# Two layers of a diffusion trunk on one Trainium2 core: where experts stand in the passes, how tokens are gathered, and which ScalarE tables are loaded

## What is computed

```python
def hier_moe(h, w_rg, b_rg, w_re, b_re, w_g, w_u, w_d):      # x: 256 tokens x 1024
    g_prob = softmax(x @ w_rg + b_rg); p_group, g_idx = top_k(g_prob, 1)          # 4 groups
    e_in = the 8 logits of (x @ w_re + b_re) in that group
    top_p, top_i = top_k(softmax(e_in), 2)                                        # 2 experts of 8
    gates = one_hot(ids) * (top_p / sum(top_p) * p_group)                         # 256 x 32
    hid = silu(einsum("nd,edf->nef", x, w_g)) * einsum("nd,edf->nef", x, w_u)     # f = 256
    y = einsum("nef,efd->nd", hid * gates[:, :, None], w_d)
```

## Time and profile before

| | us |
|---|---|
| median of 3 runs | 956.28 (954.70 to 958.65) |
| the profiled execution | 955.08 |
| its span, first to last instruction | 953.3 |
| PE busy | 824.9 (87%) |
| DVE busy | 350.6 (37%) |
| ACT busy | 203.9 (21%) |
| POOL busy | 37.5 (4%) |
| moved by DMA | 291.60 MB, mean 306 GB/s |

### The profile page before, as it was taken

The page is one execution under the profiler, slowest core; times in us unless marked ns, Lnnn a source line. Parts: engine busy times, 40 slices in busy tenths (PEclk is TensorE's granted clock), DMA queues, the critical chain, the costliest instruction groups (busy, mean ns, idle before and its releaser), DMA issues.

```text
span 953.3 us, 17639 instructions
## 1 busy us (share of the span) xinstructions
PE 824.9 (87%) x7754; PEld 550.4 (58%) x7754; DVE 350.6 (37%) x682; ACT 203.9 (21%) x360; POOL 37.5 (4%) x33
## 2 busy tenths in 40 slices
PE   4799999889996999898786789999599988978665
PEld 3687676778896464363343264898546444533324
DVE  0255567224236434232423231233543432341323
ACT  2215222233351111111111040304121111111103
POOL 0000010101004000000000000000400000000000
PEclk9999999999997999899988889999599998998886
DMA  9973345849994998999999999820089799999931
GB/s 341 378 262 108 111 139 206 299 179 282 398 402 192 371 379 323 414 417 414 419 413 419 393 386 395 353 89 1 0 350 388 314 415 418 414 420 413 418 159 45
DMA packets 88591, 291.60 MB, mean 306 GB/s; under 512 B 10857, under 2 KB 13887, under 8 KB 72127
## 3 DMA queue, kind: packets, MB, share of 16 engines
q1 hardware_dynamic: 77984, 284.70, 76.2%
q10 hardware_dynamic: 10527, 5.73, 2.1%
HBM read 288.31 MB, written 2.10 MB: 305 GB/s over the span
## 4 chain that ended last, share of the span: by engine, by line
PE 65%; DMA 21%; SPq 5%; DVE 4%; ACT 2%; issue 2%; ACTq 1%; DVEq 0%
DMA ring<-in_w_exp_up 14%; PE psum L1197 13%; PE psum L1121 6%; PE psum L798 6%; DMA scratch<-in_w_exp_up 5%; PE psum L1215 5%; PE psum L830 4%; PE psum L1187 4%; PE psum L1226 4%; PE psum L888 3%; PE psum L744 3%; PE psum L1323 3%; PE psum L1336 3%; SPq L606 2%; DMA ring<-in_w_in_even 2%
## 5 line engine op out<-in xcount | busy, mean ns | idle before, releaser
L1197 PE MATMUL psum<-scratch 128*32 128x512 f32 (+2 forms) x528 | 151.9, 665 | 32.6 <-DMA ring<-in_w_exp_up 26.4
L1197 PE MATMUL psum<-ring,scratch 128*32 128x512 f32 (+2 forms) x528 | 134.8, 656 | 23.1 <-DMA scratch<-in_w_exp_up 19.3
L1197 PEld LDWEIGHTS psum<-scratch 128*32 128x32 f32 (+2 forms) x528 | 43.9, 136 | 111.8 <-issue 111.7
L1226 PE MATMUL psum<-scratch 128*128 128x256 bf16 x576 | 70.4, 281 | 9.8 <-DVE scratch L2195 9.8
L1197 PEld LDWEIGHTS psum<-ring,scratch 128*32 128x32 f32 (+2 forms) x528 | 38.2, 129 | 69.2 <-issue 69.2
L1226 PEld LDWEIGHTS psum<-scratch 128*128 128x128 bf16 x576 | 56.3, 101 | 36.1 <-issue 16.9
L1187 PE MATMUL psum<-scratch 128*128 128x128 bf16 x1152 | 73.0, 227 | 2.7 <-DVE scratch L2179 2.7
L1187 PEld LDWEIGHTS psum<-scratch 128*128 128x128 bf16 x1152 | 70.8, 102 | 3.0 <-issue 2.8
L1652 ACT ACTIVATE scratch<-psum 128x256 f32<-128x256 f32 x24 | 9.2, 384 | 261.0 <-PE psum L1197 261.0
L798 PE MATMUL psum<-hT,ring 128*128 128x256 f32 x256 | 57.4, 387 | 2.4 <-DMA ring<-in_w_in_even 2.4
L2199 DVE TENSOR_TENSOR scratch<-psum,scratch 128x256 f32<-128x256 f32 x24 | 10.2, 424 | 125.1 <-ACT scratch L1652 125.0
(11 more groups left out here) (313 smaller groups left out, 1039.9 us busy)
## 6 DMA issues: line engine op xcount, KB each, us to landing
ring<-in_w_mod SPq DMA_DIRECT2D x42, 1024.0 KB, 8.8
scratch<-in_w_exp_gate SPq DMA_DIRECT2D x32, 1024.0 KB, 15.9
scratch<-in_w_exp_up SPq DMA_DIRECT2D x32, 1024.0 KB, 18.1
scratch<-in_w_exp_down SPq DMA_DIRECT2D x32, 1024.0 KB, 21.1
ring<-in_w_exp_gate SPq DMA_DIRECT2D x32, 1024.0 KB, 17.4
ring<-in_w_exp_up SPq DMA_DIRECT2D x32, 1024.0 KB, 18.9
ring<-in_w_exp_down SPq DMA_DIRECT2D x28, 1024.0 KB, 20.4
ring<-in_w_in_even SPq DMA_DIRECT2D x14, 1024.0 KB, 15.0
```

The lines of the kernel that those rows point to most:

```text
L1197: last = mm(bank[0][i * m:(i + 1) * m, :], xg[:, k, i * m:(i + 1) * m], w[e][:, k, :, :], start=(k == 0), stop=(k == KT - 1))
L1226: last = mm(bank[4 + k // 2][:, (k % 2) * T:(k % 2 + 1) * T], y3[:, j, k, :], ohT, start=False, stop=True, skip_group_check=True)
```

## The change

- NFIX goes from 4 to 6: experts 0 to 5 have fixed places in the first three pairs. The order of the passes changes from pair, pair, mono, quad, pair, quad, pair, three, pair, quad, pair, quad to pair, pair, pair, quad, pair, pair, quad, mono, quad, pair, three, quad. All 32 experts are still loaded, in 49 chunks; SP waits for the router ahead of q == 3.
- The gather multiplies float32 rows (hrow) by a float32 one-hot matrix: 8 matmuls for each half. The second copy on ACT and all of POOL's splitting are gone.
- ACT loads one common table for Ln and Exp (roots), and Silu's or Gelu's ahead of their use (gates, preload_act_table). Line numbers shift by a few; those of the profile before are used here.

```diff
-NFIX = 4
+NFIX = 6
-RANK2 = 10
+RANK2 = 8
-PASSES = [("pair", [("e", 0), ("e", 1)], 0), ("pair", [("e", 2), ("e", 3)], 4), ("mono", [("r", 0)], 8),
-          ("quad", [("r", 12 + i) for i in range(4)], 32), ("pair", [("r", 1), ("r", 2)], 12),
-          ("quad", [("r", 16 + i) for i in range(4)], 36), ("pair", [("r", 3), ("r", 4)], 16),
-          ("three", [("r", 9), ("r", 10), ("r", 11)], 28), ("pair", [("r", 5), ("r", 6)], 20),
-          ("quad", [("r", 20 + i) for i in range(4)], 40), ("pair", [("r", 7), ("r", 8)], 24),
-          ("quad", [("r", 24 + i) for i in range(4)], 44)]
+PASSES = [("pair", [("e", 0), ("e", 1)], 0), ("pair", [("e", 2), ("e", 3)], 4), ("pair", [("e", 4), ("e", 5)], 8),
+          ("quad", [("r", 10 + i) for i in range(4)], 32), ("pair", [("r", 1), ("r", 2)], 16),
+          ("pair", [("r", 3), ("r", 4)], 20), ("quad", [("r", 14 + i) for i in range(4)], 36), ("mono", [("r", 0)], 12),
+          ("quad", [("r", 18 + i) for i in range(4)], 40), ("pair", [("r", 5), ("r", 6)], 24),
+          ("three", [("r", 7), ("r", 8), ("r", 9)], 28), ("quad", [("r", 22 + i) for i in range(4)], 44)]
...
-                    if q == 2:
+                    if q == NFIX // 2:
                         sp.wait_ge(S.v_pos, 3 * l + 3)
...
-                        for j in range(3):
-                            last = mm(bank[b][:, k * P:(k + 1) * P], h3[j][:, t, half * 4 + k, :], Pm[:, t, :],
-                                      start=(t == 0 and j == 0), stop=(t == 1 and j == 2))
+                        last = mm(bank[b][:, k * P:(k + 1) * P], hrow[:, t, half * 4 + k, :], Pm[:, t, :],
+                                  start=(t == 0), stop=(t == 1))
...
-                pe.wait_ge(S.g_h, 6 * l + 6)
...
+            def roots():
+                nc.scalar.preload_act_table_set("natural_log_exp_and_others")
+            def gates():
+                nc.scalar.preload_act_table(ACT.Silu)
...
+            gates()
             gate_silu(6)
             columns_copy(0, 5)
             columns_copy(1, 4)
             gate_silu(7)
+            roots()
             columns_copy(2, 5)
...
-                    A(hrow[:, t, :, at], src, ACT.Copy)
-                    A(h3[0][:, t, :, at], src, ACT.Copy).then_inc(S.a_hr, 1)
+                    A(hrow[:, t, :, at], src, ACT.Copy).then_inc(S.a_hr, 1)
...
+            roots()
             act.wait_ge(S.t_ws, 1)
             A(wsT[:, :, :].rearrange("p g n -> p (g n)"), bank[4], ACT.Copy).then_inc(S.a_ws, 1)
...
-            for l in range(DEPTH):
-                for t in range(NB):
-                    n = 6 * l + 3 * t
-                    pool.wait_ge(S.a_hr, 4 * l + 2 * t + 2)
-                    nc.gpsimd.tensor_tensor(hrow[:, t], hrow[:, t], h3[0][:, t], ALU.subtract).then_inc(S.g_h, 1)
-                    pool.wait_ge(S.g_h, n + 1)
-                    pool.tensor_copy(h3[1][:, t], hrow[:, t]).then_inc(S.g_h, 1)
-                    pool.wait_ge(S.g_h, n + 2)
-                    nc.gpsimd.tensor_tensor(h3[2][:, t], hrow[:, t], h3[1][:, t], ALU.subtract).then_inc(S.g_h, 1)
```

More of the change, by code:

```diff
@@ L195, in __init__ @@
         self.g_bm = sem("g_bm")
-        self.g_h = sem("g_h")
         self.g_v1 = sem("g_v1")
@@ L433, in build @@
         bsp = part(10240, (4, P))
-        hrow = part(0, (NB, KT, P))
         xg = part(0, (KT, 2 * CAP))
@@ L441, in build @@
         pgT = part(2816, (T,))
-        Pm = scratch[:, 3072:3200].bitcast(BF16).rearrange("p (t s) -> p t s", t=NB)
-        ohT = scratch[:, 3200:3200 + T // 2].bitcast(BF16)
+        Pm = part(3072, (NB, 2 * CAP))
+        ohT = scratch[:, 10144:10144 + T // 2].bitcast(BF16)
         PG = part(3328, (NB, 2 * CAP))
@@ L448, in build @@
         R0 = 6688
-        h3 = [scratch[:, at:at + NB * D // 2].bitcast(BF16).rearrange("p (t k n) -> p t k n", t=NB, k=KT)
-              for at in (8096, 9120, 10144)]
+        hrow = part(8096, (NB, KT, P))
         more = [scratch[:, 11360 + i * SLOT:11360 + (i + 1) * SLOT] for i in range(MORE)]
@@ L1696, in layer_norm_scale @@
                     A(vsq, vtk[:, t, :], ACT.Square, accum_out=lns[:, t:t + 1]).then_inc(S.a_sqv, 1)
+                roots()
                 act.wait_ge(S.a_sqv, 2)
                 inv_root(lnr, lns, 1.0 / D, S.a_lnr, 1)
+                nc.scalar.preload_act_table(ACT.Gelu_apprx_tanh)
+            roots()
             stream_squares(3, sqo)
```

## The result

The changed kernel takes 933.37 us, median of 4 runs (930.75 to 933.93), beside 957.27 us (954.70 to 958.65) of the kernel before. The ratio is 0.9753, with an interval of 0.9721 to 0.9785. Measured again (e9), beside 954.41 us of the kernel before, it came out at 0.9791 (0.9757 to 0.9825). The profiled execution of the first took 933.48 us, its span 931.7 against 953.3 before: 21.6 us less, where the sum said 22.0. The sum is right, but several of its parts are not.

What follows compares the result with a forecast made beforehand. Bound by PE and DVE up to the first up projection, three passes at PE's pace, then DMA's bytes. Terms for routers, clock and first gathers, passes and tables summed to -22.0 from 955.1, so 933.1; forecast median 934, range 924 to 943.

Steps and rivals of the forecast that it cites:

- The passes: Each layer's mixture: 3 MiB more put in DMA's holes, 7.7 us, less 2.7 for three dearer gathers, gains 5.0 us.
- the condition of the prefetch: In the mixtures' DMA: the passes' gain needs chunks 6 and 7 loaded ahead of the router's end.
- The routers: Both layers' routers: without POOL's work DVE's slow two-input instructions speed up, gaining 5.6 us in layer 0, 4.5 in layer 1.
- The clock in layer 0: Layer 0's count and first gather: PE's clock stays whole, gaining 1.7 us in the gather and 1.2 in counting.
- clock low in layer 0 as well: Rival at layer 0's count and first gather: PE's clock is halved there too, 939 us in all; chance 0.14.
- layer 0's first term: From the start to layer 0's first up projection: the sum had 7.4 us less.
- The middle: From the start of layer 0's last up projection to layer 1's first: the sum had 3.3 us less.
- The tail: From layer 1's last up projection to the end: 1.3 us less, as the Exp's load in the last root goes.
- The tables: ACT's table loads: 21 go, saving 1.3, 0.6, 0.3 and 0.5 us on the path; two added ones cost 1.4 each.
- POOL was not the cause: Rival in the routers: the slow DVE instructions stay, 10.1 us less gained, 944 us; chance 0.05.
- the passes give nothing: Rival in the mixtures: slots free late or a DMA hole opens, the sum loses 10 us, 944 us; chance 0.08.
- a gather takes 7.2 us: Rival, the slower side: every pass's float32 gather runs at the half clock price, 970 us in all; chance 0.03.

Runs made afterwards that it cites:

- e9: The changed kernel itself, unaltered, timed once more beside the kernel before: 936.05 us, ratio 0.9791.
- e1: The kernel before with only the new order of passes; bf16 gather, POOL's splitting and own table loads stay: 938.81 us, ratio 0.9860.
- e2: The changed kernel with the old order of passes (four fixed places): 946.99 us, ratio 0.9921 to the kernel before.
- e6: The changed kernel with SP waiting for the router ahead of pass 2 again, so chunks 6 and 7 aren't loaded ahead: 935.36 us, ratio 0.9796.
- e3: The kernel before with only the float32 gather, no second copy and no POOL splitting; old order and own tables: 946.12 us, ratio 0.9916.
- e10: The changed kernel with its two added common table loads moved behind other copies, timed a second time: 928.64 us, ratio 0.9724.
- e8: The changed kernel with its two added common table loads moved behind other copies, first timing: 928.43 us, ratio 0.9725.
- e4: The changed kernel without loads, each activation loading its own table, 37 loads again: 930.48 us, ratio 0.9770.
- e7: The changed kernel with unused matmuls keeping PE busy, 6 (layer 0) or 20 (layer 1) ahead of the count, 5 behind: 935.25 us, ratio 0.9803.
- e11: The changed kernel with both added table loads moved and 3 (layer 0) or 13 (layer 1) unused matmuls ahead of the count, 5 behind: 925.57 us, ratio 0.9706.

## Why the prediction was right, and where not

**The passes (-5.0, -5.0; measured -5.3, -6.3): right, with its mechanism.** Gather 3.57 us, quad done at 59.2, 58 MiB behind it in 150.6 and 149.5 us, which is 2.60 and 2.58 us per MiB. e1 and e2 show the order's share as 6.4 to 8.2 us (7.7 in the sum). The three dearer gathers cost 1.1 to 2.0 us, not 2.7. Only the condition of the prefetch was wrong (e6). One reading was loose: of the 6.3 us of holes "just ahead of pass 3's up projection" the larger part lies in the stretch from 740 us, and so in the main during it (741.89 to 748.89). The ledger goes by the end of the up projection and isn't touched.

**The routers (-5.6, -4.5).** The DVE chain shrank as forecast: from the last router matmul to the count 9.48 to 5.02 us in layer 1, -4.5. In layer 0 it is 10.60 to 6.51, -4.1. DVE was done at 296.73 there, but PE, whose L1153 began at 298.28, waited 1.5 us longer:

```profile
298.28 0.63 PE L1153 MATMUL psum<-scratch,const 128*128 128x32 f32 x4 [2.00 <-issue]
```

"Issue" says that the profile shows nothing that it waited for. The gap is there in e3, e6 and e10 too (1.9 to 2.0 us), and missing in e8 and e9, which are the same code as e10 and the changed kernel and waited the 0.51 us of the forecast: it comes and goes between executions of equal code, with a router of 6.5 or of 5.0 us. In e2 and e4 it is 5.7 and 5.8 us. Its cause stays open.

**The clock in layer 0 (-1.7 -1.2; measured +0.7 -0.8): wrong.** The rival "clock low in layer 0 as well" held. The step that failed is that an idle time ahead of the count cut to half a microsecond would keep the clock whole. In this execution the idle time was 2.0 us, not 0.5, and PE's stretches show the clock fall during the count, to 1.2 GHz, half of 2.4, and stay there into the first gather:

```profile
296.00:298.00 2.00, 0.28 (x12) 0.00 (x0) 1.73 (x14) 1.36 (x2) 0.00 (x0) 1.00 1.00 401
298.00:300.00 2.00, 1.72 (x14) 1.66 (x14) 0.43 (x3) 0.73 (x2) 0.00 (x0) 0.79 1.03 416
300.00:302.00 2.00, 0.66 (x5) 0.61 (x5) 1.58 (x8) 0.00 (x0) 0.00 (x0) 0.50 1.05 432
302.00:304.00 2.00, 2.00 (x12) 2.00 (x11) 0.67 (x3) 0.00 (x0) 0.00 (x0) 0.50 1.01 422
```

But the low clock doesn't need the gap. In e9 the idle time was 0.51 us, as forecast, and the clock whole through the count; it fell in the gather instead, which took 5.44 us (the same in e8):

```profile
303.00:306.00 3.00, 1.52 (x14) 1.39 (x14) 2.64 (x17) 2.08 (x3) 0.00 (x0) 1.00 1.02 419
306.00:311.00 5.00, 4.68 (x27) 4.71 (x28) 2.43 (x10) 0.00 (x0) 0.00 (x0) 0.66 1.02 424
```

Between count and gather PE waits 1.3 to 1.4 us more for the one-hot matrix, which the prediction left out of its idle time. e3 and e10, with the gap of 1.9 to 2.0 us ahead of the count and a whole clock through it, have 5.44 and 5.40 as well, so there the gap makes no difference to the gather. In layer 0 of e7 and e11, 1.96 and 1.64 us of idle time stayed ahead of the added matmuls, and only 0.16 and 0.15 us ahead of the gather, which took 3.81 us at the whole clock. So what the prediction missed is the wait between count and gather. No run fills that wait alone. In layer 1 the low clock and the 6.0 us were forecast, and 5.99 came.

**The start of layer 0, which the sum left alone (+3.0).** Of this 1.4 is the added load at 140.88, as forecast. Another 1.4 was there at L846 (103.08 for 101.69), where PE's code is still the same as before and only ACT's table loads differ: PE's L740 at 30.82, behind a wait for DMA, ran at half the clock, and PE began L794 2.3 us later than before. Executions of equal code differ here by more. From 84 to 88 us PE does nearly the same work (L812 and L819) in e11 (first row) and in e9 (second), and the two kernels have the same code up to there:

```profile
84.00:88.00 4.00, 4.00 (x23) 3.61 (x23) 2.96 (x13) 0.82 (x5) 0.00 (x0) 1.00 1.04 400
```

```profile
84.00:88.00 4.00, 4.00 (x21) 3.78 (x21) 1.04 (x6) 0.40 (x1) 0.00 (x0) 0.61 0.97 359
```

Between L812 and L846, some 20.8 us of PE's work in e11, e9 lost 3.3 us there. The first up projection of layer 0 came at 308.4 and 312.7 in the changed kernel, at 306.1 and 309.7 in e8 and e10. Yet it isn't shown that the start is scatter alone. L846 began at 101.2 to 102.2 in the four kernels with their own table loads (before, e1, e3, e4), and at 101.95 to 106.4 in the nine profiles with the common table; no run settles whether the early table loads have a part in it. The four misses of layer 0's first term (+1.9 start, +1.5 gap, +2.4 clock of the gather, +0.4 counting, less 0.2 behind it) are 6.0 us together. Of these the gap comes and goes with the execution and isn't the change's; for the start this stays open.

**The middle (-3.3; measured -5.3).** Router -4.5 and gather +0.9 came as forecast. The added load cost 1.4 and, in this execution, 1.6 more, since the clock halved behind it (L1343 took 5.46 us for 3.84); e9 has the load's wait without that. Against it the matmuls of the second half's router ran at the whole clock, 1.96 us for 3.61 before, and from the first half's matmuls to theirs it was 4.96 us for 6.65, with two table loads fewer on the way: -3.3, of which the sum had 0.5. That makes -3.9; the other -1.4 holds the 0.6 of L1323 and is otherwise not taken apart.

**The tail (-1.3; measured -3.3).** The Exp's load of 1.28 us is gone. The last up projection took 9.02 us for 9.86, and the rest of the tail, some 1.2 us less, I did not take apart.

**The tables (+0.1 net): right in sum and in both added loads,** 1.43 us at L906 (1.82 for 0.39) and 1.42 at L1343 (2.16 for 0.74). e4 shows the net as none, and e8 and e10 show that moving the two added ones gains. The prediction's sign of being wrong, "PE waiting over 1.5 us at either added load", was badly chosen: both waits are above it, and its own sum (0.39 + 1.4 and 0.74 + 1.4) has them there.

So 934 came true by luck, with errors that cancel: about 6 us too much in layer 0's start, some 2 us too little each in the middle and the tail, 1.6 in the passes. The range of 924 to 943 held also the second measurement. The rivals that POOL was not the cause, that the passes give nothing and that a gather takes 7.2 us have fallen; the rival of a low clock in layer 0 held.

## What to carry to other kernels

In a stream of loads through a fixed number of slots, write a ledger: how many bytes are in when the step that frees the next slot ends, and what a byte costs from there. An order that puts more bytes ahead of that step gains just these bytes' time, while a prefetch still further ahead gains nothing once they fit. Keep POOL off the path of small two-input DVE instructions, and put a table load where no engine waits for what follows it: 21 loads saved and two badly placed ones came to nothing here, and moving the two gave some 3 us or more.

## What the runs showed of the hardware

- A two-input DVE instruction waits for the whole POOL instruction beside it and ends some 0.08 us behind it, at 1.04 us as at 1.89; a reduce beside the same instruction takes its 0.22 us.
- The granted clock falls to half in short pieces of a single core's program and differs there between executions of equal code: 1.00 against 0.61 from 84 to 88 us, 3.3 us over some 21 us of PE's work. With the other differences the end of layer 0's router came at 291.8 to 298.3 us in three profiles of the same code up to there (changed, e7, e9). So a term of some 2 us there can't be read off one pair of profiles.
- Added matmuls cost what they last beyond the input that PE waits for: 20 of them, 1.6 us too long, gave away half of the 3.4 us won in layer 1's router and gather; with 13 the count came only 0.1 us later.
- ACT's first activation behind a table load starts 0.02 us after it, and the engine that waits for it waited 1.42 and 1.43 us longer for a load of 1.28.
